# Transposes moved ahead of the value products, and the shared expert's sums stored from ScalarE's queue

## The reference, cut to what matters

```python
scores = einsum('bnqhgd,bnkhd->bnhgqk', qc, kb) * ATTN_SCALE
p = sink_softmax(where(valid, scores, -inf), sinks)          # e / (sum(e) + exp(sink - m))
o = einsum('bnhgqk,bnkhd->bnqhgd', p, vb)
...
ffn = swiglu(hf, w_sh_gate, w_sh_up, w_sh_down)              # shared expert
    + routed_experts(hf, top_idx, top_w, w_gate, w_up, w_down)  # 64 experts, 8 per token
```

## Time and profile before

| what | value |
|---|---|
| median of 3 runs | 2415.61 us (2411.41 to 2418.85) |
| the profiled execution's own time | 2420.74 us |
| its span, first to last instruction | 2419.0 us |
| mean granted TensorE clock | 0.971 |
| granted clock, 1360 to 1372 us of the span | 0.50 |
| busy: PE, PEld, DVE, ACT, POOL | 92%, 74%, 50%, 40%, 19% |
| attention stage | about 265 to 402 us of the span |
| experts' stage | about 1339 to 2370 us |

### The profile page before, as it was taken

The page is one execution under the profiler, slowest core; times in us unless marked ns, Lnnn a source line. Parts: engine busy times, 40 slices in busy tenths (PEclk is TensorE's granted clock), DMA queues, the critical chain, the costliest instruction groups (busy, mean ns, idle before and its releaser), DMA issues. The chain is left out here.

```text
span 2419.0 us, 43465 instructions
## 1 busy us (share of the span) xinstructions
PE 2237.2 (92%) x12706; PEld 1791.0 (74%) x12707; DVE 1200.6 (50%) x2074; ACT 971.8 (40%) x1740; POOL 457.2 (19%) x520
## 2 busy tenths in 40 slices
PE   6999798999999989999999799999999999999880
PEld 2444466999999989995558378888888778788760
DVE  3332476111232223122557256567777767677855
ACT  2201487111111112110320356566767667677752
POOL 0000100000000000000000023344554444445540
PEclk9999899999999999999999899999999999999995
DMA  9420000111211101115310578888989988899956
GB/s 360 178 80 0 16 1 19 45 42 41 73 44 43 43 1 52 43 35 214 132 60 1 217 261 239 256 251 299 303 278 289 308 285 293 274 303 292 315 171 252
DMA packets 140764, 387.65 MB, mean 160 GB/s; under 512 B 21004, under 2 KB 80980, under 8 KB 113060
## 3 DMA queue, kind: packets, MB, share of 16 engines
q1 hardware_dynamic: 110500, 307.02, 34.5%
q0 software_dynamic: 30032, 79.16, 13.8%
q10 hardware_dynamic: 176, 0.75, 0.1%
HBM read 350.46 MB, written 70.07 MB: 174 GB/s over the span
## 5 line engine op out<-in xcount | busy, mean ns | idle before, releaser
L1904 DVE TENSOR_TENSOR ex_wgu_lo<-ex_stage_gu,ex_wgu_hi (+1 forms) x256 | 296.8, 1221 | 77.2 <-ACT ex_wgu_hi L1824 77.0
L1755 PE MATMUL ex_pgu<-ex_wgu_hi,ex_xT_hi 128*128 (+1 forms) x784 | 318.2, 406 | 11.3 <-DVE ex_xT_lo L1916 10.8
L1755 PE MATMUL ex_pgu<-ex_wgu_hi,ex_xT_lo 128*128 (+1 forms) x784 | 310.1, 396 | 0.0
L1755 PE MATMUL ex_pgu<-ex_wgu_lo,ex_xT_hi 128*128 (+1 forms) x784 | 309.7, 395 | 0.0
L1824 ACT CAST ex_wgu_hi<-ex_stage_gu (+1 forms) x256 | 249.6, 1047 | 45.2 <-DMA ex_stage_gu<-in_w_exp_up 25.6
L1678 POOL DMA_INDIRECT sum_rows<-ex_y,ex_index_scatter x98 | 165.8, 1692 | 392.9 <-issue 314.1
L886 PE MATMUL cv_ph<-fourth_r,cv_split 128*128 128x272 f32 x1536 | 225.9, 289 | 4.0 <-DVE cv_split L935 4.0
L886 PEld LDWEIGHTS cv_ph<-fourth_r,cv_split 128*128 128x128 f32 x1536 | 206.4, 189 | 4.1 <-DVE cv_split L935 4.1
L1692 POOL DMA_DIRECT2D ex_rows<-h_rows x2 | 1.1, 550 | 1065.9 <-issue 1065.9
L411 PE MATMUL qk_pp<-early_late,hT 128*128 128x512 f32 (+1 forms) x432 | 190.8, 595 | 0.0
L1755 PEld LDWEIGHTS ex_pgu<-ex_wgu_hi,ex_xT_hi 128*128 128x128 f32 x784 | 149.0, 190 | 44.2 <-issue 12.7
(11 more groups left out here) (294 smaller groups left out, 4005.1 us busy)
## 6 DMA issues: line engine op xcount, KB each, us to landing
ex_stage_gu<-in_w_exp_gate SPq DMA_DIRECT2D x64, 1024.0 KB
ex_stage_gu<-in_w_exp_up SPq DMA_DIRECT2D x64, 1024.0 KB, 10.0
ex_stage_dn<-in_w_exp_down SPq DMA_DIRECT2D x64, 1024.0 KB, 7.3
fourth<-in_w_ada SPq DMA_DIRECT2D x24, 1024.0 KB, 8.9
w_ahead<-in_w_in SPq DMA_DIRECT2D x24, 512.0 KB, 3.7
early_late<-in_w_in SPq DMA_DIRECT2D x16, 512.0 KB, 3.7
early_late<-in_w_in SPq DMA_DIRECT2D x3, 2048.0 KB, 14.1
n_work<-in_x_prompt POOLq DMA_DIRECT2D x8, 512.0 KB, 9.3
```

Source lines behind the costliest of these rows:

```text
L1755: last = pe.matmul(pgu[:, :], xT[a][:, k, :], w, start=(k == 0 and (a, c) == PASSES[0]), stop=(k == KT - 1 and (a, c) == PASSES[-1]))
L1904: dve.tensor_tensor(gu_piece(1, slot, q), gu_raw(slot, q), gu_piece(0, slot, q).bitcast(F32), ALU.subtract).then_inc(gu_lo, 1)
```

## The change

In attention, PE's loop becomes `scores(u+2)`, `transposes(u)`, `values(u-1)`. At the start of the experts' stage, the nine stores leave SP's stream; ACT issues each of them on its own queue right behind the two copies, after a wait for these copies to be done. `split_gu(0, 0)` moves from behind tile 3 to behind tile 6, and `split_dn(0, 0)` from behind tile 5 to behind tile 8.

```diff
@@ attention, PE
                     for u in range(len(units)):
                         if u + 2 < len(units):
                             scores(u + 2)
+                        transposes(u)
                         if u:
                             values(u - 1)
-                        transposes(u)
                     values(len(units) - 1)
@@ experts, SP
                     for p in range(3):
                         sp.wait_ge(w_loaded[p], 16)
                         load(p, second, 1)
-                    for t in range(NT):
-                        R = rows_of(t)
-                        sp.wait_ge(sh_out, 2 * t + 2)
-                        sp.dma_start(self.sum_rows[t * P:t * P + R, :], y[t % 2][:R, :, :].rearrange("p a n -> p (a n)")).then_inc(sh_stored[t % 2], 16)
                     with sp.Fori(0, NE - 2) as i:
@@ experts, ACT
                         for j in range(2):
                             act.wait_ge(sh_down, 2 * t + j + 1)
                             act.copy(y[t % 2][:R, j, :], psh[t % 2][j][:R, :]).then_inc(sh_out, 1)
+                        act.wait_ge(sh_out, 2 * t + 2)
+                        act.dma_start(self.sum_rows[t * P:t * P + R, :], y[t % 2][:R, :, :].rearrange("p a n -> p (a n)")).then_inc(sh_stored[t % 2], 16)
 
                     for t in range(NT):
                         shared_out(t)
-                        if t == 3:
+                        if t == NT - 3:
                             split_gu(0, 0)
-                        if t == 5:
-                            split_dn(0, 0)
+                    split_dn(0, 0)
                     columns(0)
                     split_gu(1, 1)
                     split_dn(1, 1)
```

## The result

The changed kernel takes 2412.19 us (median of 20 runs, 2399.09 to 2422.39), the kernel before, run beside it, 2423.79 us (20 runs, 2411.41 to 2435.30). The ratio is 0.9949, 95% interval 0.9935 to 0.9964: faster by 0.51%, 12.4 us (8.7 to 15.7). The forecast was faster by 17 us, to 2399 us; 2412.19 lies above the upper end of its range, 2410.

What follows compares the result with a forecast made beforehand. Attention was taken as bound by PE with waits for ACT's copy, the experts' start by stores late in SP's stream. -7 and -10 made -17 us: 2420.7 to 2404 on the profiled execution, 2399 on the median; range 2388 to 2410.

Steps and rivals of the forecast that it cites:

- Attention, -7: Attention: with transposes ahead of values, PE no longer waits for ACT's copy; 7 us less, bounds 0 and -12.
- The round of four units: Attention: three units at PE's 3.31 us, the fourth waiting 0.77 us for DVE; 14.0 instead of 14.9 us.
- (a): Attention: every unit, not each fourth, waits for DVE's `tail`; only -10 remains, 2406 us; chance 0.12.
- At the end the waits of 1.15 us go: End of attention: three waits of 1.15 us vanish, since values of the unit in front cover the copy.
- -12, if the split finds a gap: Attention's upper bound: DVE's split_h finds a gap, so 30 units save 0.40 us each.
- Stores, -10: Start of the experts' stage: block 1's first product at 1389.3 instead of 1399.13, 10 us less; bounds -13 and -3.
- 1.3 us of fixed time ... makes 6.7: Stores on ACT's queue: 5.4 us for 0.52 MB at 97 GB/s plus 1.3 us fixed, 6.7 us per store.
- 150 GB/s: Stores on ACT's queue: the rate after POOL's gathers end at about 1355, with SP's queue alone beside it.
- PE ... waits 1 us in all: Nine shared tiles: PE, two tiles ahead, waits 1 us in all and ends them at 1371.5.
- (b): Stores still land after 9.3 us, only issued earlier; -3 here, -7 from attention, 2406 us; chance 0.13.
- (c): Later in the experts' stage some wait absorbs the stores' gain; only -7 remains, 2409 us; chance 0.10.
- (d): ACT's queue starves at 46 GB/s, so stores last until 1441 and delay block 1: 2451 us; chance 0.03.

Runs made afterwards that it cites:

- order alone: The kernel before with only attention's new PE order, the stores staying with SP: ratio 0.9985 to the kernel before.
- after: The changed kernel itself, with both parts of the change, against the kernel before: 2412.19 us, ratio 0.9949.
- the split ahead of `head`: The changed kernel with DVE's split_h ahead of head(u+2) in every fourth unit of attention: ratio 0.9930 to the kernel before.
- after once more: The changed kernel, nothing edited, profiled in one further execution: 2408.97 us.
- the late weights: The changed kernel with SP's loads of the second expert's weights held back until tile 5's copies are done: ratio 0.9952 to the kernel before.
- the splits back: The changed kernel with split_gu(0,0) and split_dn(0,0) back behind tiles 3 and 5: ratio 0.9976 to the kernel before.
- four buffers: The changed kernel with four SBUF buffers instead of two for the shared expert's sums: ratio 0.9922 to the kernel before.

## Why the prediction was right and wrong

Both places and the direction were right. Three numbers failed: how long a store takes to land beside loads, what the end of attention gives, and the level from which the gain was taken off.

**Attention, -7: the rounds right, the ends not.** The round of four units was forecast at 14.0 us and is 14.03; the wait for DVE comes once in four units, at the split. Rival (a), a wait in every unit, is out. At the same clock at both ends (order alone against before) the gain is 7.5, of which the rounds give 5.7 (units 3 to 32 take 101.4 us instead of 107.2); 6 were forecast. That the sum came so near is in part luck. The end was to give 3.4 us and the start to lose about as much; the start up to unit 3 gave 0.8, and the end, from unit 32 on, 1.0. After itself got 5.8. What failed there is the sentence "At the end the waits of 1.15 us go": they went, but unit 32 waits 1.44 us, and in after the clock then fell. What makes it fall is open. Behind the same wait it fell to 0.50 until the end of attention in after, after once more, the late weights and the splits back, for 3.4 us with four buffers (1.00 again from 394 us on), and not in the order alone. In the first four the clock had been 1.00 from 15 to 20 us behind the first scores, in the other two 0.50; no run tests whether that matters. The bound "-12, if the split finds a gap" was passed: with the split ahead of `head` the gain is 14.6.

**Stores, -10: sign and place right, size too large; 6.7 measured.** The term that failed is "1.3 us of fixed time ... makes 6.7": the first store landed after 10.1 us, because it moved one packet in its first 4 us. The rate beside two loaded queues was right, 0.40 MB in 4 us against 97 GB/s; tiles 0 and 1 landed 5.0 us apart, as forecast (1351 and 1356). Behind the gathers 150 GB/s was too much: the next two landed 4.2 and 4.5 us apart, 125 and 116 GB/s. So "PE ... waits 1 us in all" became 4.2. The full clock forecast for all nine tiles also failed: the first tile's products took 5.35 us, 3.69 in before, so the first store was issued some 1.5 us later than the forecast has it. Block 0 hangs on ACT: the copies of tile 6 were to end 28.2 us behind the first shared product and ended at 32.4, and from there to block 0 it took 11.5 us, as forecast. These 4.2 us are the whole delay of block 0 (43.93 instead of 39.8). From block 0 to the third row transposes 1.1 us came back.

**The rivals.** (a) is told above. (b) was half right: the stores landed as late as on SP's queue (10.1 and 11.7 us against 9.7), and yet 6.7 us came, not 3. By the rule of the Trainium skill named there only issue time is saved; here that was time in an ordered stream, 13 us for the first store. The Trainium skill (DMA: Bandwidth & Descriptors, "Queues, rings and completion order") also says that each DMA engine takes turns between its queues by whole packets. The trace agrees where all queues move: 113, 112 and 114 packets, as the profile counts them, from three queues in 4 us. It does not show turns in the 4 us before, in which the issued store moved one; why, no run here shows. (c), given back later, is out for the whole of the stage's gain: without it 5.8 us would be left, and the timed gain is 12.4 (8.7 to 15.7); that a small part came back is not excluded. The last stretch alone (1012.6 us before, 1012.3 in after, 1015.4 in after once more) would not settle it. (d) is out: the last store landed at 1379.6, ahead of block 1's first product at 1388.24.

**The level.** Of the 13.2 us between 2399 and 2412.19, 8.2 are the level of before: the forecast took 17 off the median of three runs, 2415.61, and before's median over 20 runs is 2423.79. The range's upper end allowed for a smaller gain, not for the level. That single executions differ by some us where nothing was edited (937.1 and 934.0, 1012.3 and 1015.4) could not be read from one trace; the three times, 2411.41 to 2418.85, hinted at it. The remaining 5 us are the two terms, 3.3 of the stores and 1.2 of attention; the rest is rounding and within the timing's interval.

## What to carry to other kernels

When a store shares the DMA engines with large loads, look at packets: beside loaded queues its bytes went by the size of its packets, and its first packet came 4 us late. More buffers hid both here, although the stores landed later still. When two groups change places to cover a wait, follow the other engine's order through its longest round: here one subtraction in front of `tail` cost 8.8 us of attention, about half of it by the lower clock at the end, more than the 5.8 that the swap brought. The narrower a forecast's range, the more runs its level needs.

## What was not expected of the hardware

- A 512 KB store issued at 1339.99 beside loads that held 96.4% of the DMA engines moved one packet until 1344, and one of 256 KB issued at 1373.27 beside a load moved next to nothing until 1377.4; with no load under way a 512 KB store lands in 2.6 us.
- Queues that are all loaded got equal numbers of packets (113, 112, 114; later 162 and 164), not equal bytes.
- Behind one and the same wait of 1.44 us the granted clock was 0.50 to the end of attention in four executions, 0.50 for 3.4 us in one, and 1.00 in one. The price at the end was up to 4.6 us (14.21 against 9.65).
- The first eight shared products took 5.25 to 5.39 us in after and in all experiments, behind the same 2.9 us of idle time as in before's profiled execution, where they took 3.69. In after the clock was 0.50 for the first 3.4 us of them. The one trace of before did not show that this tile usually runs slow.
